# A two-layer hybrid decoder step on one core: page gathers that wait for a sample's exponentials, and recurrence outputs and states in PSUM banks by even and odd head tiles

## The chip, the core and the metric

The kernel runs on one core of one Trainium2 chip. The metric is the device time of one execution in microseconds; the time stated for a kernel is the median of its executions. All arithmetic is fp32.

## What is computed

One inference step of a decoder of 2 layers (width 1024) runs for two groups of tokens at once: a prompt of 256 tokens, and 8 samples of 8 new tokens each, every sample with 2048 past tokens in caches. Each layer is: half a SwiGLU feed-forward block (inner width 2816), a token mixer with three branches, and another half feed-forward block, with RMSNorm around each. Two places of the mixer matter here.

```
# A: RWKV-7 recurrence, 8 heads x 64, with a matrix state s[value, key] per head
def step(s, inp):
    r_t, w_t, k_t, v_t, kk_t, a_t = inp
    sa = einsum('bhvk,bhk->bhv', s, -kk_t)
    s = s * w_t[:, :, None, :] + sa[..., None] * (kk_t * a_t)[:, :, None, :] + v_t[..., None] * k_t[:, :, None, :]
    return s, einsum('bhvk,bhk->bhv', s, r_t)

# C: latent attention, 8 heads; a sample's past latents are paged rows of a pool
ckv  = cache_mla_ckv[l][page_table].reshape(8, 2048, 256)      # latent rows
kr   = cache_mla_krope[l][page_table].reshape(8, 2048, 32)     # rotated keys
s    = (q_lat . ckv + q_rope . kr) * scale                     # 64 rows (8 heads x 8 tokens) x 2048 keys, and 8 own keys
o    = softmax(s) @ ckv
```

Branch B is a dilated window attention over cached keys and values. The new caches, the states and the outputs of both groups are returned.

## The kernel before, in words

Five engines run programs of their own, tied by counted semaphores: TensorE (PE in the profile), VectorE (DVE), ScalarE (ACT), GpSimd (POOL) and SyncE (SP). All matmuls are issued by one helper, `mm` (L787), and all transposes on PE by another, `tr` (L790), so their rows have these lines and are told apart by the names of what they read. SP loads the weights into three slots of `ring`; POOL copies the window caches to the outputs (L722) and issues the page gathers (L740, L744). The order on each engine is the order of the program.

**The recurrence** (PE: `rwkv`, L1023; DVE: L2487 to L2502; ACT: L1866 to L1891). The prompt's 256 tokens are worked in 4 chunks of 64 tokens (g = 0 to 3); a fifth unit holds the samples. Round r of the loop at L1052 builds the products of chunk r and finishes chunk r - 1: `rhs`, `solve` and `outputs` (L1205). Every matmul there is 64 x 64 by 64 columns, on one quarter of the array: `times` (L510) and `beside_each_other` (L1095) pair head tiles so that four quarters work at a time, while `each` (L1088) uses two. Between these steps `fill(n)` (L1002) issues n of the 168 steps of the projections of the other branches (a step is 128 x 128 by 512 columns, or two of half the width for the sample tokens), so that PE has work while DVE and ACT answer. `FILL_STEP` is 2.

`outputs(g)` for g < 4 makes two results for each of 4 head tiles m and both 64-row halves: y (what the chunk puts out) and h (what is added to the state). Before, y is in bank 4 and h in bank 5. The state's part of y comes first, for all tiles and with no wait; then PE waits for U (`u_ev`, from DVE's `u_out`, L2594), multiplies y of even and h of odd tiles, does one step of filling, waits for its own counter `across` (so that two row halves never add to the same bank at once), and does h of even and y of odd tiles. Then it increments `h`. On that, DVE adds h to the state `Hp` and decays it (`state`, L2597 to L2602), and ACT copies y out (L1880, which increments `y_out`). The next `rhs` (L1163) waits for both.

**The latent attention of the samples** (PE: `ml_sample`, L1567; DVE: L2883; ACT: L2037 and L2051; POOL: L746 to L772). One sample b takes one round:
- PE multiplies the scores, `ml_scores(b)` (L1502): 4 steps of low keys, 4 of high keys and 1 of rotary keys, all in 32-row strips. `ml_mm` is incremented after step 5 and after step 8, so it is 2b + 1 within the high keys and 2b + 2 at the end. Then come the result of sample b - 2 by channel, the own tokens of b + 1 (`ml_s`), the products with the values of b - 1 (`ml_pv`), and transposes of the shares of b (`ml_PT`).
- DVE waits for `ml_mm` 2b + 2 and takes the maximum straight from 4 PSUM banks (L2896); four tiny instructions make the bias (L2897 to L2900, `ml_nm`). Then it takes the own scores of b + 1 (L2889), transposes the low keys of sample b + 1 (L2838, `keys`, L2840; these wait for that sample's pages), copies the result of b - 2 (L2922) and the own share (L2908), transposes the high keys of b + 1, and makes the divisor.
- ACT takes the exponentials when `ml_nm` says so (L2042, then L2044 with the increment of `ml_exp`), and copies the transposed shares (L2063).
- POOL gathers the pages of sample b in two halves of 1 MB (L744) and one of rotary keys, 128 KB (L740), into the buffer b modulo 4. For b = 2 and 3 it waits for `ml_mm` to reach b (that is: sample 0's scores are done; sample 1's high keys are under way). From b = 4 on it waits for `ml_pv` b - 3 (the buffer is free) and for `ml_mm` 2(b - 2) + 1 (sample b - 2's high keys are under way). The pages of samples 0 and 1, and the rotary keys of sample 3, are gathered earlier. The second half of sample 2 also waits for the gates' products (`pgm` 24).

`spot`, `spots` and `paired` (L514 to L521) already exist and are used by `rhs` and for the samples: `spot(R, m, at)` is in bank 4 for even m and in bank 5 for odd m.

## Time and profile before

| | us |
|---|---|
| median of 3 executions | 2506.28 |
| lowest and highest | 2504.1, 2511.38 |
| the profiled execution's own time | 2509.38 |
| its span, first to last instruction | 2507.6 |
| PE busy in the span | 2457.0 |
| DVE busy | 1303.8 |
| ACT busy | 562.0 |
| POOL busy | 67.7 |

All times of rows are from the span's start. "Busy" for PE is the time in which a matmul was under way as recorded; the starts of matmuls are recorded, their ends are modelled. `<-remote` behind a wait means that a semaphore's last increment fits no recorded end of an instruction. The mean granted TensorE clock is 0.998 of full speed. The recurrence's chunks run at about 380 to 470 us in layer 0 and 1710 to 1790 us in layer 1, the samples' latent attention at about 850 to 947 and 2093 to 2190 us.

### The profile page before, as it was taken

The page shows a single profiled execution, that of the slowest core. Times are in us where ns is not written, and L with a number is a line of the kernel's source. Part 1 is how long each engine was busy: PE and PEld are TensorE (multiplying, and loading weights), DVE is VectorE, ACT ScalarE, POOL GpSimd, SP SyncE. Part 2 cuts the span into 40 slices and gives each one's busy share as a digit, 9 for nine tenths or more (in the row PEclk, how much of TensorE's full clock was granted, in tenths as well). Part 3 has the DMA queues.
Part 4 walks back from the last instruction along what each step waited for, and adds up shares of the span by engine and source line. Part 5 has one row for each costly group of instructions (what it writes and reads, how often), then busy time and mean ns, then how long its engine had stood idle before and what let it go on. Part 6 is the DMA issues. An engine that isn't in the chain of part 4 may idle for free.

```text
span 2507.6 us, 52981 instructions
## 1 busy us (share of the span) xinstructions
PE 2457.0 (98%) x23140; PEld 2023.9 (81%) x23140; DVE 1303.8 (52%) x2829; ACT 562.0 (22%) x1233; POOL 67.7 (3%) x92
## 2 busy tenths in 40 slices
PE   8999999999999999999999999999999999999998
PEld 7999956666767778999999998566667667799998
DVE  5663554445543563766376545543465335537654
ACT  2110231133432222111121102311344222231111
POOL 0000000000000110000000000000000002000000
PEclk9999999999999999999999999999999999999999
DMA  8767662143986554666856686522549864446775
GB/s 276 248 187 249 215 226 69 53 155 139 394 322 238 159 197 130 202 205 212 262 183 208 209 259 227 166 69 69 182 170 400 293 209 158 179 132 202 235 215 158
DMA packets 260853, 505.59 MB, mean 202 GB/s; under 512 B 9808, under 2 KB 198736, under 8 KB 245648
## 3 DMA queue, kind: packets, MB, share of 16 engines
q1 hardware_dynamic: 251920, 330.77, 40.0%
q0 software_dynamic: 8704, 171.45, 19.0%
q8 instruction: 183, 3.00, 0.5%
q14 instruction: 46, 0.38, 0.0%
HBM read 491.89 MB, written 140.85 MB: 252 GB/s over the span
## 4 chain that ended last, share of the span: by engine, by line
PE 86%; DVE 5%; DMA 4%; ACT 2%; another core or an unknown queue 1%; issue 1%; PEld 1%; SPq 0%; DVEq 0%; ACTq 0%
PE ps L787 82%; PE ps L790 4%; DMA big<-in_cache_swa_k_dram 3%; DVE big L2838 1%; DVE ring L2838 1%; DMA ring<-in_w_in_dram 1%; DVE sml L2896 1%; PEld ps L787 1%; DVE reg L2165 0%; ACT big L1990 0%; DVE reg L2239 0%; ACT reg L1990 0%; DVE x L2157 0%; ACT reg L1931 0%
## 5 line engine op out<-in xcount | busy, mean ns | idle before, releaser
L787 PE MATMUL ps<-reg 128*128 128x160 f32 (+13 forms) x4584 | 504.6, 292 | 1.6 <-DVE reg L2244 1.6
L787 PEld LDWEIGHTS ps<-reg 128*128 128x128 f32 (+5 forms) x4584 | 448.8, 162 | 29.6 <-issue 22.7
L787 PE MATMUL ps<-reg,ring 128*128 128x160 f32 (+2 forms) x3072 | 457.0, 305 | 1.8 <-issue 1.8
L787 PE MATMUL ps<-h,ring 128*128 128x320 f32 (+2 forms) x1984 | 445.7, 376 | 10.9 <-ACT h L1717 8.3
L787 PEld LDWEIGHTS ps<-reg,ring 128*128 128x128 f32 (+1 forms) x3072 | 427.4, 189 | 13.0 <-issue 2.6
L787 PEld LDWEIGHTS ps<-h,ring 128*128 128x128 f32 (+1 forms) x1984 | 322.7, 189 | 98.9 <-issue 22.4
L787 PE MATMUL ps<-ring,h 128*128 128x512 f32 (+3 forms) x896 | 247.0, 468 | 0.0
L787 PEld LDWEIGHTS ps<-big,ring 128*128 128x128 f32 (+2 forms) x1888 | 191.7, 170 | 24.8 <-issue 20.5
L787 PE MATMUL ps<-big,ring 128*128 128x160 f32 (+2 forms) x1888 | 208.4, 284 | 0.5
L787 PEld LDWEIGHTS ps<-ring,h 128*128 128x128 f32 (+1 forms) x896 | 101.8, 163 | 79.9 <-issue 64.8
L787 PE MATMUL ps<-big,reg 32*64 32x256 f32 (+8 forms) x2144 | 130.8, 350 | 1.5 <-DVE big L2838 1.3
L787 PEld LDWEIGHTS ps<-big,reg 32*64 32x64 f32 (+4 forms) x2144 | 99.5, 133 | 27.8 <-issue 15.7
L790 PE MATMUL ps<-cst,big 128*128 128x128 f32 (+1 forms) x672 | 95.2, 281 | 12.6 <-DMA big<-in_cache_swa_k_dram 6.4
L790 PEld LDWEIGHTS ps<-cst,big 128*128 128x128 f32 (+1 forms) x672 | 72.3, 140 | 28.1 <-DMA big<-in_cache_swa_k_dram 8.8
L1827 ACT ACTIVATE reg<-ps 128x320 f32<-128x320 f32 x40 | 17.5, 437 | 316.3 <-PE ps L787 316.3
L787 PE MATMUL ps<-ys,ring 128*128 128x320 f32 x256 | 75.4, 440 | 1.3 <-ACT big L1942 1.2
L787 PEld LDWEIGHTS ps<-big 64*64 64x64 f32 (+1 forms) x1536 | 51.6, 134 | 29.8 <-issue 29.0
L2389 DVE TENSOR_TENSOR ys<-ys,ps 128x320 f32<-128x320 f32 x40 | 19.5, 487 | 107.8 <-PE ps L787 107.7
L787 PEld LDWEIGHTS ps<-ring 128*16 128x16 f32 (+3 forms) x1888 | 59.2, 111 | 15.3 <-issue 15.2
L787 PE MATMUL ps<-ring 128*16 128x128 f32 (+3 forms) x1888 | 71.2, 261 | 0.2 <-issue 0.2
L787 PE MATMUL ps<-ring,reg 32*64 32x256 f32 (+2 forms) x1312 | 70.5, 374 | 0.0
L1830 ACT ACTIVATE ys<-reg 128x640 f32<-128x640 f32 x40 | 29.5, 737 | 181.3 <-DVE reg L2409 181.3
(335 smaller groups left out, 2677.4 us busy)
## 6 DMA issues: line engine op xcount, KB each, us to landing
out_o_swa_k_s_dram<-in_cache_swa_k_dram POOLq DMA_DIRECT2D x16, 4080.0 KB, 15.7
out_o_swa_v_s_dram<-in_cache_swa_v_dram POOLq DMA_DIRECT2D x16, 4080.0 KB, 15.2
ring<-in_w_in_dram SPq DMA_DIRECT2D x30, 2048.0 KB, 8.8
ring<-in_f_wd_dram SPq DMA_DIRECT2D x32, 1408.0 KB, 7.6
ring<-in_f_wg_dram SPq DMA_DIRECT2D x42, 1024.0 KB, 5.7
ring<-in_f_wu_dram SPq DMA_DIRECT2D x42, 1024.0 KB, 8.7
big<-in_cache_swa_k_dram SPq DMA_DIRECT2D x32, 1024.0 KB, 8.9
ring<-in_cache_swa_v_dram SPq DMA_DIRECT2D x32, 1024.0 KB, 7.4
```

The costliest lines, as they stand in the source:

```text
L787: return pe.matmul(out, lhsT, rhs, start=first, stop=last, skip_group_check=True)
L790: return pe.transpose(out, in_, ident[0:rows, 0:rows])
L1827: act.activation(GU[u % 2][:, :, 0, 0:HT], summed(X), ACT.Copy).then_inc(S["gu_act"], 1)
L1830: act.activation(SG[u % 2], GU[u % 2][:, 0], ACT.Sigmoid).then_inc(S["ffn_sg"], 1)
L2389: dve.tensor_tensor(Vs, Xc, Y, ALU.add).then_inc(S["gu_sum"], 1)
L2838: dve.transpose(out, pages).then_inc(S["ml_keys"], 1)
L2896: link(dve.tensor_reduce(sml[:, 0:1], ps[:, 0:4, 0:256], mybir.AxisListType.XY, ALU.max))
```

## The change

POOL: the gathers of sample b >= 2 wait for the exponentials of sample b - 2 (`ml_exp` is b - 1 when ACT is through with them) in place of a count of the score matmuls. The wait for `ml_pv` from b = 4 on stays.

The recurrence: y and h lie in banks 4 and 5 by even and odd tiles (y from column 256, h from column 384). The state's part of y now comes behind the wait for U, odd tiles first; `across` is incremented after the odd ones, four matmuls before the end of that group; PE waits for it, and then does all parts of h and of y without a step of filling between. The step of filling goes to the `fill` behind `outputs`. ACT's copy of y waits for DVE's `state` in place of `h`. DVE reads h through the paired view.

```diff
@@ POOL, the gathers of sample b @@
                     elif b in (2, 3):
                         pool.wait_ge(S["prompt_y"], 2 * H)
                         pool.wait_ge(S["ml_prep"], 1)
-                        pool.wait_ge(S["ml_mm"], b)
+                        pool.wait_ge(S["ml_exp"], b - 1)
                     else:
                         pool.wait_ge(S["ml_pv"], b - 3)
-                        pool.wait_ge(S["ml_mm"], 2 * (b - 2) + 1)
+                        pool.wait_ge(S["ml_exp"], b - 1)
@@ PE, the rounds of the recurrence @@
                     if r:
                         outputs(r - 1)
-                    fill(FILL_STEP - FILL_STEP // 2 if 0 < r < 5 else FILL_STEP)
+                    fill(FILL_STEP)
                     if r < 5:
                         blocks(r)
@@ PE, outputs(g) for g < 4 @@
-                y, h = [lambda R, m, bank=bank: ps[R, bank, col(m, at=256)] for bank in (4, 5)]
-                y_of_u = lambda R, Q, m: mm(y(R, m), U[Q, m], RB[i][Q, m], False, False)
-                y_of_v = lambda R, Q, m: mm(y(R, m), VB[i][Q, m], KKRK[i][Q, m, CHUNK:], False, True)
-                h_of_u = lambda R, Q, m: mm(h(R, m), VB[i][Q, 4 + m], U[Q, m], m < 2, False)
-                h_of_v = lambda R, Q, m: mm(h(R, m), KDr[i][Q, m], VB[i][Q, m], False, True)
-                each(lambda R, m: mm(y(R, m), Hp[R, m], RqT[R, m, t], m == 0, False))
                 pe.wait_ge(S["u_ev"], g + 1)
-                beside_each_other(y_of_u, h_of_u)
-                beside_each_other(y_of_v, h_of_v).then_inc(S["across"], 1)
-                fill(FILL_STEP // 2)
+                for m in (1, 3, 0, 2):
+                    for r in range(2):
+                        R = channels(r)
+                        q = mm(spot(R, m, 256), Hp[R, m], RqT[R, m, t], m < 2, False)
+                    if m == 3:
+                        q.then_inc(S["across"], 1)
                 pe.wait_ge(S["across"], ACROSS["outputs", g])
-                beside_each_other(h_of_u, y_of_u)
-                beside_each_other(h_of_v, y_of_v).then_inc(S["h"], 1)
+                y_of_u = lambda R, Q, m: mm(spot(R, m, 256), U[Q, m], RB[i][Q, m], False, False)
+                y_of_v = lambda R, Q, m: mm(spot(R, m, 256), VB[i][Q, m], KKRK[i][Q, m, CHUNK:], False, True)
+                h_of_u = lambda R, Q, m: mm(spot(R, m, 384), VB[i][Q, 4 + m], U[Q, m], False, False)
+                h_of_v = lambda R, Q, m: mm(spot(R, m, 384), KDr[i][Q, m], VB[i][Q, m], False, True)
+                for part in (h_of_u, h_of_v, y_of_u, y_of_v):
+                    q = beside_each_other(part, part)
+                q.then_inc(S["h"], 1)
@@ ACT @@
                     if 1 <= r < 5:
-                        act.wait_ge(S["h"], g + 1)
-                        act.activation(S_[8][:, :, g * CHUNK:(g + 1) * CHUNK], ps[:, 4, 256:512].rearrange("p (m t) -> p m t", m=4), ACT.Copy).then_inc(S["y_out"], 1)
+                        act.wait_ge(S["state"], g + 1)
+                        act.activation(paired(S_[8][:, :, g * CHUNK:(g + 1) * CHUNK]), spots(256), ACT.Copy).then_inc(S["y_out"], 1)
@@ DVE @@
             def state(g):
                 dve.wait_ge(S["h"], g + 1)
-                link(dve.tensor_tensor(Hp, quarter(5, 256), Hp, ALU.add))
+                link(dve.tensor_tensor(paired(Hp), spots(384), paired(Hp), ALU.add))
```

## Rows read from the trace of the kernel before

**Rows 1.** The page: the chain that ended last, by engine.

```profile
PE 86%; DVE 5%; DMA 4%; ACT 2%; another core or an unknown queue 1%; issue 1%; PEld 1%; SPq 0%; DVEq 0%; ACTq 0%
```

**Rows 2.** Windows, core 0: us, PE, PEld, DVE, ACT, POOL busy, PEclk, DMA share, GB/s.

```profile
396.00:470.00 74.00, 73.38 (x1346) 47.19 (x1345) 33.42 (x103) 10.90 (x23) 0.00 (x0) 1.00 0.23 80
851.10:928.40 77.30, 72.90 (x1364) 55.73 (x1365) 59.97 (x137) 21.95 (x56) 16.00 (x17) 1.00 0.58 209
2094.20:2174.40 80.20, 74.38 (x1364) 57.49 (x1363) 59.94 (x137) 22.09 (x56) 16.00 (x17) 0.98 0.56 202
```

**Rows 3.** DVE's waits over the whole span: us in total, times, longest.

```profile
DVE sml L2896 <- remote: 23.2, 9, 4.3
```

**Rows 4.** Timeline, layer 0, samples 3 and 4: start us, us, engine, line.

```profile
883.28 0.64 PE L787 MATMUL ps<-big 32*64 32x256 f32 x16
883.47 0.94 POOL L744 DMA_INDIRECT reg<-in_cache_mla_ckv_dram,pidx  x1 [8.36 <-PE ps L787]
884.71 0.93 POOL L744 DMA_INDIRECT reg<-in_cache_mla_ckv_dram,pidx  x1 [0.30 <-issue]
885.60 1.23 DVE L2896 TENSOR_REDUCE sml<-ps 128x1 f32<-128x1024 f32 x1 [2.35 <-remote]
897.36 1.23 DVE L2896 TENSOR_REDUCE sml<-ps 128x1 f32<-128x1024 f32 x1 [2.32 <-remote]
```

**Rows 5.** Timeline, layer 0, samples 0, 6 and 7, no gather begun before.

```profile
850.39 0.64 PE L787 MATMUL ps<-big 32*64 32x256 f32 x16
851.13 1.22 DVE L2896 TENSOR_REDUCE sml<-ps 128x1 f32<-128x1024 f32 x1 [3.80 <-PE ps L787]
917.88 1.22 DVE L2896 TENSOR_REDUCE sml<-ps 128x1 f32<-128x1024 f32 x1 [0.77 <-PE ps L787]
920.04 2.37 DVE L2838 STREAM_TRANSPOSE ring<-ring 128x1024 f32<-128x1024 f32 x2
928.42 1.22 DVE L2896 TENSOR_REDUCE sml<-ps 128x1 f32<-128x1024 f32 x1 [1.43 <-PE ps L787]
```

**Rows 6.** Timeline, layer 0, sample 0: ends of exponentials, a gather, ACT beside it.

```profile
854.39 0.19 ACT L2044 ACTIVATION_READ_ACCUMULATOR ring<-ring,sml 64x1 f32 x1
855.26 0.94 POOL L744 DMA_INDIRECT h<-in_cache_mla_ckv_dram,pidx  x1 [1.17 <-PE ps L787]
856.06 0.60 ACT L2063 ACTIVATE reg<-ps 128x512 f32<-128x512 f32 x1 [0.51 <-PE ps L790]
```

**Rows 7.** The gathers' lines (L744, then L740), from issue to landing.

```profile
DMA to landing us min/median/max: 5.6/7.0/9.4
...
DMA to landing us min/median/max: 5.0/6.7/7.7
```

**Rows 8.** Timeline, layer 0: the low keys of sample 2.

```profile
864.79 1.25 DVE L2838 STREAM_TRANSPOSE ring<-ring 128x1024 f32<-128x1024 f32 x1 [0.30 <-DVE ring L2889]
```

**Rows 9.** PE's timeline, chunk 0 of layer 0: from before outputs to behind it.

```profile
404.14 1.98 PE L787 MATMUL ps<-ring,h 128*128 128x512 f32 x4
407.44 0.57 PE L787 MATMUL ps<-reg,big 64*64 64x64 f32 x14
408.47 1.12 PE L787 MATMUL ps<-ring,h 128*128 128x512 f32 x2
409.53 0.27 PE L787 MATMUL ps<-big,ring 64*64 64x64 f32 x2
411.21 0.68 PE L787 MATMUL ps<-big,ring 64*64 64x64 f32 x16
```

**Rows 10.** PE's timeline, chunk 0 of layer 0: rhs, with its wait inside.

```profile
399.82 0.63 PE L787 MATMUL ps<-ring 64*64 64x64 f32 x16
400.29 0.46 PE L787 MATMUL ps<-big,reg 64*64 64x64 f32 x16
```

**Rows 11.** Timeline, chunk 0 of layer 0: DVE's U, and ACT's next wait behind y.

```profile
404.33 0.42 DVE L2594 TENSOR_SCALAR big<-ps 128x256 f32<-128x256 f32 x1 [0.79 <-PE ps L787]
414.93 0.38 ACT L1885 ACTIVATE big<-ps 128x256 f32<-128x256 f32 x1 [4.26 <-PE ps L787]
```

## The prediction

> **What bounds the kernel now.** I read the chain first: 86% of it is PE [rows 1], so whatever makes PE's work shorter counts, and elsewhere only what keeps PE waiting. Then the windows of the two stages that the change touches [rows 2]. In the recurrence PE is busy for 73.38 of 74 us, with DVE at 33.42: PE is the bound, and only its own time counts. In the samples' latent attention, from the first maximum (L2896) to the eighth, a layer takes 77.3 us and the other 80.2, and PE, with 72.90 and 74.38, isn't quite the bound. Something else sets the pace there.
>
> DVE's waits name it [rows 3]: L2896 waited 9 times, 23.2 us in all, for something "remote", that is for an increment that fits no end of a matmul. The timeline shows one [rows 4]: the last score matmuls begin at 883.28 and end 0.64 later, at 883.92, but the maximum begins at 885.60, 1.7 us behind. Where no gather has just begun it doesn't wait like this [rows 5]: the same matmuls from 850.39 end at 851.03, and the maximum starts 0.10 later. In between lies POOL: its two latent gathers were issued at 883.47 and 884.71 [rows 4], and the second is over at 885.64, as the maximum starts (0.04 off; samples 1 to 4 of layer 0 and 1 to 5 of layer 1 are alike, the nine of rows 3). The maximum stands in a ring: maximum, low keys, high keys, scores, next maximum. So I take it that PE's increment reaches DVE late while gathers are being issued, and that each time costs about 1.6 us. The pace agrees: 885.60 to 897.36 is 11.76 us [rows 4], and without gathers 917.88 to 928.42 is 10.54 [rows 5].
>
> **The gathers, part by part.** Now a sample's gathers begin within the scores of sample b - 2, just ahead of the critical increment. Afterwards they begin when ACT's exponentials end, 854.58 where the maximum began at 851.13 [rows 5, 6]: 3.45 us behind a maximum. POOL then issues until about 7 us behind it (three, 1.24 apart [rows 4]), and the next critical increment comes 10 us behind it.
>
> Removed: the late start, nine times. The trace has the new place once: a gather is issued at 855.26, until 856.20, and ACT's copy of the transposed shares, released by PE's increment, starts at 856.06 with no such delay [rows 6]. If an increment there came late, it would be that of the shares' transposes; ACT's copy is needed only one score group later, some 6 us, which covers it.
>
> Added: the pages are asked for later, and the low keys (DVE, in order, with high keys, own share and divisor queued behind, and PE's scores waiting for them) need them 2.16 us behind the next maximum (917.88 to 920.04 [rows 5]). The rotary gather is third, 2.5 us behind the first, and lands 5.0, 6.7 or 7.7 us after its issue (minimum, median, maximum [rows 7]), so a set lands L = 7.5, 9.2 or 10.2 us after it begins. From the low keys to the next maximum are 8.38 us (920.04 to 928.42 [rows 5]). Two samples then take at least 3.55 + 9.2 + 8.38 = 21.1 us, 10.6 each, beside the 10.54 of PE and DVE without gathers: the two limits meet, and I take 10.55. With 10.2 it is 11.1; with 7.5 the undisturbed 10.5 stays, and at best somewhat less.
>
> Sample 2 is the tight one. Before, its low keys began at 864.79, after a wait of 0.30 [rows 8]. Afterwards its rotary keys are asked for at 854.7, the second latent half 2.5 us later, at 857.2, and that lands 5.6, 7.0 or 9.4 us later [rows 7]: 862.8, 864.2 or 866.6. With the median the keys begin at 864.2, and the maximum of sample 2 comes some 8.0 us later (the 8.38 is from a round in which PE had a full load), at 872.2. Five more at 10.55 end at 925.0, against 928.42: 3.4 us gained in layer 0. Layer 1 has the same work: from 80.2 to 73.9 (925.0 less 851.1), 6.3 gained. It was longer because one more sample was delayed and because its clock stands at 0.98 [rows 2], 1.6 us of full clock lost; I assume that this dip came from the stalls and goes. In all 9.7 us. Bounds: with all the longest landings 2.4 are lost at sample 2 and 2.8 in five rounds, a layer, so 9.7 - 10.4 = -0.7; with the shortest, and rounds of 10.0, 9.7 + 2 x (1.2 + 2.8) = 17.7. After the eighth maximum the same chain follows and simply starts earlier.
>
> A rule of the Trainium skill speaks against the removal: by "SBUF — State Buffer", section "Who interferes with whom", a VectorE reduction never contends with GpSimd on this chip, and TensorE and ScalarE wait for nobody. By it the coincidence in [rows 4] would be no cause and the gathers' part would be worth 0. The trace so far stands against it with the 1.7 us beside 0.10; it is a rival below.
>
> **The recurrence, part by part.** The number of matmuls and of filling steps is the same. What goes is one interruption of each `outputs`, in 4 chunks of 2 layers, 8 times. A fill of one step occupies PE for 1.12 us, one of two steps for 1.98 [rows 9]: 2 x 1.12 - 1.98 = 0.26 saved. Going into and out of a fill once less saves some 0.05 more, as the first small matmuls behind one last 0.27 [rows 9]. Added is PE's wait for its own `across` with only four matmuls behind the increment. `rhs` has the same pattern: its first 16 records start at 399.82 and those behind the wait at 400.29 [rows 10], 0.47 us for 16, or 0.03 each, with the wait hidden within; for the slower first pair behind it I take 0.05. Net 0.26, say 0.25, of the 3.77 from 407.44 to 411.21 [rows 9], so 8 x 0.25 = 2.0 us. Bounds: the wait drains a matmul of 0.27 each time, 0; or it is free, 0.31 x 8 = 2.5, which I widen to 3.
>
> At nothing: the wait for U now stands ahead of the state's part; U is out at 404.75 (404.33 + 0.42 [rows 11]), 2.7 us ahead of 407.44 [rows 9]; without that cover it would cost what U is late. ACT's wait for `state` is about 0.9 us longer (two adds or multiplies of DVE), but `h` comes about 1.1 earlier, without the fill before it; and ACT's next wait lasts 4.26 us [rows 11]. DVE's state starts earlier; its own next wait for `blocks` grows. Nothing on PE waits for either.
>
> **Sum.** 9.7 + 2.0 = 11.7 us against the profiled execution's own 2509.38 (span 2507.6): 2497.7. That execution is 3.1 above the median 2506.28, so on the median 2494.6; I say 2494.5.
>
> **Rivals.**
> 1. *The late start isn't POOL's.* Whatever delays the increment follows the dense scores themselves, and the maxima still start 1.7 us late; the pages land in time for rounds of 11.8. For it: sample 5 of layer 0 started in time with a gather just begun, and I don't know the mechanism. Against it: samples 0, 6 and 7, with the same matmuls and no gather, are on time. It leaves only the recurrence: 2506.3 - 2.0 = 2504.3.
> 2. *The pages come late: slower.* It decides in DVE's wait at the low keys. Rounds are as slow as before when 3.55 + L + 8.38 = 23.5, so from L = 11.6. With L = 14 (a set stuck behind another, as all landings add up) a round is 13.0, 5 x 1.2 = 6 more a layer than before, and sample 2 some 4 more: 2506.3 + 20 - 2 = 2524. Against it: the longest L by [rows 7] is 10.2, and the DMA queues are busy for 0.58 of the stage [rows 2]. It needs a landing beyond any row.
> 3. *The recurrence gains nothing*, because PE drains at `across`: 2496.5.
>
> **Numbers.** About 0.3% (7.5 us) is what a measurement of this kernel can tell from no change. Chances: my forecast 0.68; rival 1 0.16; rival 2 0.06; rival 3 0.10. Within the forecast, long landings or a dip of the clock that stays leave less than 7.5 in about one case of eight. Faster by more than 0.3%: 0.60 + 0.07 = 0.67. Within: 0.16 + 0.08 + 0.01 and part of rival 2, 0.26. Slower: 0.07, rival 2 at its full price and unforeseen waits. The range: down to 2487, most of the bounds of both parts (-17.7 and -3 would be 2485.6); up to 2504.5, to take in rival 1.
>
> **What would show it.** Right: no "remote" wait of L2896, its starts 0.1 behind the last score matmul; gathers issued about 3.5 us behind a maximum; rounds of 10.5; windows from first to eighth maximum near 74 us in both layers; from 407.44 to `blocks` about 3.5 us. Wrong: rounds still of 11.8 with POOL moved (rival 1); a wait of DVE at L2838 for a gather of over 1 us in every round (rival 2); an idle gap of PE behind the state's part of y (rival 3); a new late increment in front of ACT's L2063 that something waits for.

## The result, and the profile after

| | before | after |
|---|---|---|
| median | 2506.22 us (4 runs) | 2525.44 us (4 runs) |
| lowest and highest | 2504.1, 2511.38 | 2523.2, 2541.48 |
| profiled execution, its span | 2509.38, 2507.6 | 2523.2, 2521.4 |

The ratio is 1.0078, with a 95% interval of 1.0054 to 1.0102: slower by 19 us, where I had forecast 12 us less. Lines of the code from L1218 on stand two lines lower in the kernel after: L2896 is L2898 now, L2838 is L2840, L2889 is L2891.

First the windows of the stages of [rows 2], the latent attention again from the first maximum to the eighth (us, then PE, PEld, DVE, ACT, POOL busy, PEclk, DMA share, GB/s):

```profile
393.00:467.00 74.00, 73.32 (x1319) 47.07 (x1317) 33.44 (x102) 10.90 (x23) 0.00 (x0) 1.00 0.25 87
848.10:935.90 87.80, 77.29 (x1365) 61.42 (x1365) 60.29 (x138) 22.17 (x56) 16.00 (x17) 0.98 0.50 185
2100.80:2188.30 87.50, 77.83 (x1365) 61.73 (x1365) 60.84 (x137) 22.19 (x56) 16.00 (x17) 0.98 0.50 185
```

The stages have grown from 77.3 and 80.2 us to 87.8 and 87.5, 17.8 us together: this is where the loss is. Then the seven distances from maximum to maximum, from the timelines of both kernels (not rows, but differences of them):

```
                before                                       after
layer 0   11.2 11.5 11.8 11.8 10.6  9.9 10.5     11.5 11.9 11.8 11.8 12.6 11.9 16.3
layer 1   11.2 13.1 11.8 11.8 11.8 10.2 10.4     11.5 11.8 12.3 11.8 12.6 11.8 15.9
```

Two things stand out: the middle rounds still take 11.8 or more, and the last one takes 16. DVE's waits (total us, times, longest) name the second. In place of the "remote" of [rows 3], which is gone, there is:

```profile
DVE ring L2840 <- DMA ring<-in_cache_mla_krope_dram,pidx: 9.9, 2, 5.2
DVE ring L2840 <- DMA h<-in_cache_mla_ckv_dram,pidx: 4.5, 2, 2.3
DVE ring L2840 <- DMA reg<-in_cache_mla_krope_dram,pidx: 1.3, 2, 0.7
DVE ring L2840 <- DMA big<-in_cache_mla_krope_dram,pidx: 0.4, 1, 0.4
```

L2840 is the low keys, and all of them wait for pages: 16.1 us. The timeline of layer 0 shows the longest, that of sample 7:

```profile
912.32 0.94 POOL L744 DMA_INDIRECT ring<-in_cache_mla_ckv_dram,pidx  x1 [9.58 <-issue]
914.80 0.95 POOL L740 DMA_INDIRECT ring<-in_cache_mla_krope_dram,pidx  x1 [0.30 <-issue]
919.59 1.23 DVE L2898 TENSOR_REDUCE sml<-ps 128x1 f32<-128x1024 f32 x1 [2.75 <-PE ps L787]
926.91 2.37 DVE L2840 STREAM_TRANSPOSE ring<-ring 128x1024 f32<-128x1024 f32 x2 [5.19 <-DMA ring<-in_cache_mla_krope_dram,pidx]
935.90 1.22 DVE L2898 TENSOR_REDUCE sml<-ps 128x1 f32<-128x1024 f32 x1 [2.03 <-PE ps L787]
```

The set was asked for at 912.32 and complete at 926.83: L = 14.5 us, where the longest of before gave 10.2 [rows 7]. The DMA view of 911 to 930 us says what lay beside it (queues: packets, MB, share of 16 engines; then issues with KB and median us to landing):

```profile
q0 software_dynamic: 368, 2.36, 29.8%
q1 hardware_dynamic: 528, 2.10, 28.4%
...
big<-in_w_branch_c_dram SPq DMA_DIRECT2D x1, 2048.0 KB, 13.1
ring<-in_cache_mla_ckv_dram,pidx POOLq DMA_INDIRECT x2, 11.1
ring<-in_cache_mla_krope_dram,pidx POOLq DMA_INDIRECT x1, 12.0
```

SP's load of the branch's weights (L683, 2 MB) waits for `ml_pv` 5, which comes at 912.47, within 0.2 us of the first gather. The two shared the engines half and half. Before, the gathers had begun at 907.39, 4.9 us ahead of the load, and had landed at 917.55. While DVE waits, PE stands for 4.4 us, and right behind that its granted clock is down, at half speed (1.2 GHz) for most of the next 4 us; the last round of layer 1 is alike, with 3.9 us of standing:

```profile
930.00:934.00 4.00, 4.00 (x89) 2.70 (x96) 3.66 (x9) 0.71 (x2) 0.00 (x0) 0.58 0.01 2
```

The middle rounds are told by PE's timeline between the maxima at 883.31 and 895.09:

```profile
883.31 1.23 DVE L2898 TENSOR_REDUCE sml<-ps 128x1 f32<-128x1024 f32 x1 [2.42 <-PE ps L787]
...
887.53 0.94 POOL L744 DMA_INDIRECT reg<-in_cache_mla_ckv_dram,pidx  x1 [8.35 <-ACT ring L2046]
889.09 1.94 PE L787 MATMUL ps<-ring,reg 32*64 32x256 f32 x44
890.01 0.95 POOL L740 DMA_INDIRECT reg<-in_cache_mla_krope_dram,pidx  x1 [0.30 <-issue]
891.80 0.88 PE L787 MATMUL ps<-ring,reg 32*64 32x256 f32 x18 [0.77 <-issue]
892.53 1.32 PE L787 MATMUL ps<-big,reg 32*64 32x256 f32 x38
895.09 1.23 DVE L2898 TENSOR_REDUCE sml<-ps 128x1 f32<-128x1024 f32 x1 [2.29 <-PE ps L787]
```

The matmuls of the low keys (x44, x18) wait for nothing, yet PE starts none between 890.65 and 891.80. The stop begins 0.6 us behind the start of the third issue (890.01) and outlasts it. All ten sets of three issues (the pages of samples 2 and 4 to 7, in both layers) have this stop, 1.15 to 1.18 us between two starts, some in two pieces; the two sets of sample 3, whose rotary keys are gathered earlier and which have two issues, have none. The maxima themselves now begin 0.04 to 0.13 behind the last score matmul. The price was moved, not removed.

The recurrence did what was forecast. PE's timeline of chunk 0, for [rows 9]:

```profile
406.56 0.63 PE L787 MATMUL ps<-reg,big 64*64 64x64 f32 x16
...
408.12 1.98 PE L787 MATMUL ps<-ring,h 128*128 128x512 f32 x4
410.04 0.68 PE L787 MATMUL ps<-big,ring 64*64 64x64 f32 x16
```

From the state's part of y to `blocks` it is 3.48 us against 3.77.

**Where the 19 us are.** Page waits +16.1; ten stops in place of nine late increments, about +1.6 (each costs a round some 1.6 to 1.9, see the experiments); recurrence 8 x 0.29 = -2.3. These make +15.4. The spans of the two profiled executions differ by 13.8 (the one before took 3.2 more than its median, the one after 2.2 less), the medians by 19.2. This is an account of two traces and no proof that the terms add up; the experiments test the two large ones.

### The profile page after: what moved, and what is told of

Read it like the earlier page. It is cut to its first block, busy times and chain, and to the rows that moved or that the text cites. A ratio compares the mean times of both kernels' runs of the same rounds, so it can differ in the third digit from the quotient of the medians.

```text
span 2521.4 us, 52981 instructions
## 1 busy us (share of the span) xinstructions
PE 2461.2 (98%) x23140; PEld 2033.8 (81%) x23140; DVE 1305.8 (52%) x2829; ACT 562.2 (22%) x1233; POOL 67.7 (3%) x92
## 4 chain that ended last, share of the span: by engine, by line
PE 89%; DMA 5%; DVE 2%; ACT 2%; issue 1%; PEld 1%; POOL 0%; SPq 0%; DVEq 0%; POOLq 0%; ACTq 0%
PE ps L787 84%; PE ps L790 4%; DMA big<-in_cache_swa_k_dram 2%; DMA ring<-in_cache_mla_krope_dram,pidx 1%; DMA h<-in_cache_mla_ckv_dram,pidx 1%; DMA ring<-in_w_in_dram 1%; PEld ps L787 1%; DVE reg L2167 0%; ACT big L1992 0%; ACT reg L1992 0%; DVE reg L2241 0%; POOL ring L744 0%; DVE ring L2840 0%; DVE sml L2898 0%; ACT reg L2044 0%
## 5 line engine op out<-in xcount | busy, mean ns | idle before, releaser
L787 PEld LDWEIGHTS ps<-big,reg 32*64 32x64 f32 (+4 forms) x2144 | 105.4, 134 | 20.5 <-issue 16.0
L790 PE MATMUL ps<-cst,big 128*128 128x128 f32 (+1 forms) x672 | 95.2, 281 | 13.1 <-DMA big<-in_cache_swa_k_dram 6.9
L787 PE MATMUL ps<-ring,reg 32*64 32x256 f32 (+2 forms) x1312 | 84.4, 400 | 6.9 <-issue 6.5
L787 PEld LDWEIGHTS ps<-ring,reg 32*64 32x64 f32 (+1 forms) x1312 | 51.6, 139 | 31.7 <-issue 23.8
```

What stands on the lines that cost most here:

```text
L787: return pe.matmul(out, lhsT, rhs, start=first, stop=last, skip_group_check=True)
L790: return pe.transpose(out, in_, ident[0:rows, 0:rows])
```

## The experiments

The runs stood on five chips, here called A to E. Each ratio is against the kernel before on the same chip. Its median was there:

| chip | kernel before, us | runs |
|---|---|---|
| A | 2509.4 | experiment 1 |
| B | 2507.7 | `no_gathers_from_4`, `one_gather_from_4`, `rows_of_half_length`, `behind_own_scores` |
| C | 2509.6 | `two_gathers_from_4`, `before_no_gathers_from_4`, `pages_behind_own_scores_load_later`, `recurrence_alone_2` |
| D | 2497.9 | `own_scores_rows_of_half_length`, `halves_apart`, `halves_apart_load_later` |
| E | 2498.3 | experiment 5 |

The five kernels of experiment 2, `own_scores_rows_of_half_length` and `before_again` were run once each, for their traces.

**1. Which half, and the last pages.** Four kernels. `recurrence_alone` has only the recurrence's diff, `gathers_alone` only POOL's. The others are the kernel after with

```diff
+ last_pages_as_before
                         pool.wait_ge(S["ml_pv"], b - 3)
-                        pool.wait_ge(S["ml_exp"], b - 1)
+                        if b == 7:
+                            pool.wait_ge(S["ml_mm"], 2 * (b - 2) + 1)
+                        else:
+                            pool.wait_ge(S["ml_exp"], b - 1)
+ load_held_back
-                        sp.wait_ge(S["ml_pv"], 5)
+                        sp.wait_ge(S["ml_pv"], 6)
```

> The kernel before with the recurrence's edit alone; POOL's gathers wait for counts of the score matmuls as before. Theory A (the two parts are independent; the recurrence gives about 0.3 us in each of 8 chunks, as the offsets between the traces of before and after say, and the whole loss lies in the gathers): 2506.2 - 2.2 = about 2504, between 2503 and 2505. Rival (the recurrence's edit changes where later work lies, and some of the loss is its own): over 2506.

> The kernel before with the gathers' edit alone. Theory A: all of the loss is here, 10.4 us in layer 0 and 7.2 in layer 1 by the offsets between the two traces; with other layer-1 parts some 19 to 22 us over before: 2525 to 2528. Rival: near before, 2506, if the loss came from both together.

> The kernel after, but sample 7's gathers wait for the score matmuls of sample 5 as before (some 5 us earlier than the exponentials of sample 5). Theory A (the last round of each layer waits for these pages: DVE waited 5.2 and 4.7 us for them, PE stood idle as long, because they run at the same time as the 2 MB load of the branch's weights): these waits go, 2525.4 - 9.9 = about 2515.5, and the landing of sample 7's last page comes back to about 10 us behind the first gather. Rival (the load isn't to blame and the pages of any sample land late when asked for behind another's): the wait shrinks by less than half, over 2520.

> The kernel after, but the 2 MB load of the branch's weights waits for the values of sample 5 (ml_pv 6) in place of those of sample 4, so that it starts some 12 us later. Theory A (the load and sample 7's gathers share the DMA queues and each slows the other): sample 7's pages land some 10 us behind the first gather instead of 14.5, the waits of 5.2 and 4.7 us go, about 2515.5; the load is needed only by the branch's matmuls behind sample 7's shares. Rival 1 (the gathers are slow by themselves at this place): no change, 2525. Rival 2 (the load then comes too late for PE): PE waits for the branch's weights behind the shares, a loss there that takes back part of the gain, 2518 to 2525.

Measured: `recurrence_alone` 2504.1, ratio 0.9993 (0.997 to 1.0017); `gathers_alone` 2527.4, 1.0073 (1.0049 to 1.0098); `last_pages_as_before` 2515.38, 1.0022 (1.0004 to 1.0041); `load_held_back` 2517.71, 1.0021 (1.0003 to 1.0039). So the loss is POOL's edit alone, and the overlap of sample 7's pages with the load is about half of it: against `gathers_alone` on the same chip, and with the 2.3 us of the recurrence taken off, the two ways of parting them give back 9.7 and 7.4 us. With the load held back, sample 7's set landed 10.1 and 9.8 us behind its first issue, not 14.5. DVE's waits there:

```profile
DVE ring L2840 <- DMA ring<-in_cache_mla_ckv_dram,pidx: 4.7, 2, 2.4
```

This is what stays of page waits of over 1 us a piece; the 5.2 for sample 7 is gone (0.8 is left in layer 0). One thing more is in the trace of `last_pages_as_before`: with sample 7's set back at its old place, just ahead of a critical increment, the late increment came back too. The maximum of sample 5 begins 0.95 us behind the last score matmul in layer 0 and 2.43 in layer 1 (a round of 14.8).

**2. What keeps the round at 11.8.** The kernel after with fewer or shorter gathers for samples 4 to 7 (they work on older pages in part or whole, with DVE's counts of landings set to match):

```diff
@@ no_gathers_from_4 @@
-                for b in range(NB):
+                for b in range(4):
@@ one_gather_from_4: the first latent half alone @@
+                    if b >= 4:
+                        latents_gathered(b, 0)
+                        continue
@@ two_gathers_from_4: no rotary keys @@
-                    if b >= 4:
-                        krope_gathered(b)
@@ rows_of_half_length, in latents_gathered (cut) @@
+                    if b >= 4:
+                        short = io["cache_mla_ckv"].rearrange("l n (s r) c -> (l n s) (r c)", s=32)
+                        ... out=KRc[b % 4][half][:, 0:4, :] ...
```

> The kernel after without the gathers of samples 4 to 7: those samples work on the pages of samples 0 to 3 again, so the output is another; it is a measurement. Theory B (a gather's issuing costs PE and DVE some time in its round wherever it stands, 1.3 us a round, and this is what keeps the round at 11.8): the four rounds that no longer issue anything (from the third maximum on) take 10.0 to 10.5 us in place of 11.8 to 16, and the four late increments or stops of PE are gone. Rival (the pace of 11.8 is PE's and DVE's own and has nothing to do with gathers): these rounds still take 11.5 or more, and only the last, which waited for pages, shrinks.

> The kernel after with only the first latent half of samples 4 to 7 gathered (half the bytes, one of three issues; the rest of the pages is that of an earlier sample, so the output is another). Theory B with a price by issue: rounds lie at about 10.4 + 0.4, near 10.9. If only the third issue hurts (PE stopped 3.1 to 4.3 us behind the start of the first, when the third was being issued): 10.4, as without gathers. Rival (the bytes in flight hurt): about 11.1, half way.

> The kernel after with as many gathers as ever, at the same places, but the latent ones of samples 4 to 7 bring rows of half the length (half the bytes; the other half of the buffer keeps older data, so the output is another). Theory B (issuing hurts, bytes don't): the middle rounds stay at 11.8, PE still stops within the low keys; the last round of each layer no longer waits for its pages and also takes about 11.8. Rival (traffic hurts): the middle rounds fall to about 11.

> The kernel after without the rotary gather of samples 4 to 7 (two issues a sample in place of three, 2 MB of 2.13; the rotary keys are those of an earlier sample, so the output is another). Theory C (PE's stop within the low keys is bound to the third issue, which is under way when it begins): the stop goes, the middle rounds take about 10.2. Rival (any issue does it, the stop only comes with the second then, or the price is by the issue): the stop stays or halves, rounds of 11 or more.

> The kernel before without the gathers of samples 4 to 7 (those samples work on older pages, so the output is another). Theory B (the late increments of the kernel before are the same thing as the stops of PE in the kernel after: what POOL's issuing costs at another place): no late increment from the third maximum on, rounds of about 10.0, and the span is 2 x 4 x 1.6 us or so shorter than before, some 2497. Rival (late increments come from the dense scores): rounds of 11.8 as before.

`before_no_gathers_from_4` is the same first edit in the kernel before. The maxima of two samples without gathers, in the kernel after and in the kernel before:

```profile
886.81 1.22 DVE L2898 TENSOR_REDUCE sml<-ps 128x1 f32<-128x1024 f32 x1 [0.85 <-PE ps L787]
896.77 1.23 DVE L2898 TENSOR_REDUCE sml<-ps 128x1 f32<-128x1024 f32 x1 [0.84 <-PE ps L787]
```

```profile
2120.87 1.23 DVE L2896 TENSOR_REDUCE sml<-ps 128x1 f32<-128x1024 f32 x1 [0.84 <-PE ps L787]
2130.83 1.23 DVE L2896 TENSOR_REDUCE sml<-ps 128x1 f32<-128x1024 f32 x1 [0.84 <-PE ps L787]
```

9.96 us both times, eight rounds of the one kernel and nine of the other between 9.96 and 10.4 (2501.35 and 2496.52 us in all). Where the gathers are gone, late increments and stops are gone; the sets that are left in these two kernels still have theirs (1.7 us and 1.17, once a layer). So both are the price of gathers. With half the bytes but all three issues the stop stays (PE's timeline of `rows_of_half_length`; the third issue begins at 880.75), and the middle rounds are 11.75 to 11.87. The last ones missed their expectation with 13.9 and 12.3: sample 7's pages still made DVE wait 2.9 and 2.4 us.

```profile
879.76 1.99 PE L791 MATMUL ps<-ring,reg 32*64 32x256 f32 x44
882.52 0.89 PE L791 MATMUL ps<-ring,reg 32*64 32x256 f32 x18 [0.78 <-issue]
```

With two issues (1 MB each) it is gone, and a round without another trouble takes 10.33; with one, 10.13, in a run of 2506.91 us (`two_gathers_from_4`, DVE and PE; its lines stand lower by two):

```profile
2150.40 1.23 DVE L2896 TENSOR_REDUCE sml<-ps 128x1 f32<-128x1024 f32 x1 [3.83 <-PE ps L785]
2156.11 2.21 PE L785 MATMUL ps<-ring,reg 32*64 32x256 f32 x60
2160.73 1.23 DVE L2896 TENSOR_REDUCE sml<-ps 128x1 f32<-128x1024 f32 x1 [0.97 <-PE ps L785]
```

So it is the issuing, not the bytes, and in the low keys it is the third issue in a row. Late increments need only two: when the critical one is due, the third gather isn't yet begun [rows 4]. Yet as a whole the run with two gathers took 2521.56 us, hardly less than the kernel after: other rounds took 11.0 to 13.8, and one 15.6. Its DVE waited 11.2 us for pages, and PE had three stops of 2.2 to 2.3 us of another kind, which the third experiment shows.

**3. Another place, and a second kind of stop.** All gathers from sample 2 on wait for the own scores (`ml_s` is b). From sample 3 on their first issue comes 1.2 to 3.1 us behind a maximum, when PE is in the products with the values; sample 2's comes 5.1 behind one:

```diff
+ behind_own_scores, for b = 2, 3 and for b >= 4
-                        pool.wait_ge(S["ml_exp"], b - 1)
+                        pool.wait_ge(S["ml_s"], b)
```

> The kernel after with another place for the gathers: from sample 2 on they wait for the own scores (ml_s is b), whose increment comes about 1.2 us behind the maximum's start, so that a gather starts about 2 us behind a maximum in place of 4.2, when PE is in the products with the values and nobody waits for an increment of PE for 3 us. Theory B: the stop of PE, 3.1 to 4.3 us behind the first issue, falls on the transposes of the shares ahead of the low keys, where PE's order has no slack either: rounds stay near 11.8, but the pages come 2.2 us earlier and the waits of the last rounds shrink by as much: 2525.4 - 5 = about 2520. If the stop belongs to the low keys alone (32-row matmuls), it goes: rounds of 10.5, and with the pages of sample 7 still against the load the time is about 2505.

2511.85 us, ratio 1.0017 (1.0 to 1.0034): less gained than the better branch of the expectation, though its mechanism came out. From sample 3 on there is no stop in the low keys, and the quiet rounds take 10.11 (2151.59 to 2161.70). Sample 2's three issues still fall on low keys: there the stop stands in both layers, the granted clock is at half speed right behind it (0.51 from 858.0 to 861.5), and these first rounds take 14.0 each, against 11.2 before. On chip D the same issues stand at the same place (`own_scores_rows_of_half_length`, which shortens rows only from sample 4 on) and there is no stop; the round takes 9.6. The low keys of sample 1 in layer 1, on chip B and on chip D:

```profile
2099.41 3.23 PE L787 MATMUL ps<-ring,reg 32*64 32x256 f32 x57
2103.43 0.48 PE L787 MATMUL ps<-ring,reg 32*64 32x256 f32 x4 [0.79 <-issue]
```

```profile
2098.75 1.98 PE L791 MATMUL ps<-ring,reg 32*64 32x256 f32 x64
```

Two more rounds of layer 0 take 13.0 and 12.5. PE's timeline in the second, and the queues of 904.2 to 905.3 us:

```profile
903.62 1.28 PE L787 MATMUL ps<-big,reg 32*64 32x256 f32 x38
906.70 0.42 PE L787 MATMUL ps<-big,reg 32*64 32x256 f32 x1 [1.80 <-issue]
```

```profile
q0 software_dynamic: 92, 0.37, 85.3%
q8 instruction: 1, 0.02, 5.6%
q14 instruction: 1, 0.01, 2.1%
```

PE stops inside a step of the high keys. At 904.21 one packet of 16 KB moves in the instruction queue, until 905.20, and PE goes on 1.50 us later. The latent attention of the twenty profiles has 51 such stops of 0.8 us and more, at nine places of the program, all in the 32-row scores or within about 2 us behind them (for instance in the scores of sample 5, and behind those of sample 3), and in each a 16 KB packet ends 1.2 to 1.6 us ahead of the restart. The 1.15 us stops have, but for one, no such packet at that distance. With none of the gathers from sample 4 on, the packet of the place in sample 5's scores begins 2.6 us ahead of it and the place costs 0.2; here it began 0.3 ahead. That PE stands for its next instructions is inferred from this coincidence; no run moved the packets alone. Full queues are not the whole of it either: `no_gathers_from_4` has one such stop, of 1.01 us, in the scores of sample 7, 55 us behind the last gather, with nothing in the DMA queues between 2160 and 2165 us but two instruction packets:

```profile
2164.70 0.68 PE L787 MATMUL ps<-big,reg 32*64 32x256 f32 x14 [0.63 <-issue]
```

The kernel before has one too, in layer 1, and right behind it the granted clock is down to 0.57 for 4 us:

```profile
2106.07 0.37 PE L787 MATMUL ps<-reg,ring 128*64 128x128 f32 x2 [1.79 <-issue]
2106.44 4.82 PE L787 MATMUL ps<-big,reg 128*64 128x256 f32 x28
```

```profile
2106.00:2110.00 4.00, 3.93 (x23) 3.22 (x24) 3.81 (x10) 1.49 (x4) 0.00 (x0) 0.57 0.95 391
```

The two together are its round of 13.1. `recurrence_alone` stops at the same place for 1.5 us between two starts in place of 2.1, without a fall of the clock: its products with the values take 3.6 us in place of 4.8, and the round 11.2.

The Trainium skill ("Runtime: NRT & Kernel Launch", section "Instruction fetch mechanics") says that each engine streams its instructions by DMA in blocks of 16 KiB and that this is mostly hidden. The packets agree with the blocks; that it is mostly hidden doesn't hold for the samples' latent attention of this kernel, if the 51 stops above, from 0.8 to 3.8 us, are waits for instructions.

**4. Trying for a version that beats both.** Three placements on the kernel after, and the recurrence's half again:

```diff
+ pages_behind_own_scores_load_later: b = 2 on ml_mm b as before, else ml_s b, and
-                        sp.wait_ge(S["ml_pv"], 5)
+                        sp.wait_ge(S["ml_pv"], 6)
+ halves_apart: b = 2 as before, b = 3 on ml_s b, and for b >= 4
                         pool.wait_ge(S["ml_pv"], b - 3)
-                        pool.wait_ge(S["ml_exp"], b - 1)
...
                         latents_gathered(b, half)
+                        if b >= 4 and half == 0:
+                            pool.wait_ge(S["ml_s"], b)
```

> A version meant to beat both: the kernel after, with the gathers from sample 3 on waiting for the own scores (ml_s is b), that of sample 2 for the score matmuls as before, and the 2 MB load held to ml_pv 6. Theory B: no stop of PE in the low keys, no late increment, no page wait of sample 2 (3.8 a layer less than the run with all pages behind the own scores) nor of sample 7: 2511.9 - 2 x 2.5 - 3 = about 2504, ratio to before 0.998 or a little under. Rival (stops move to other places, such as PE's supply of instructions during the gathers): 2508 or more, ratio 1.000 or more.

> The recurrence's edit alone once more, in more rounds, beside the version above: the offset of 0.3 us in each of 8 chunks says a ratio of 0.9991; the gathers as before, so the rest is unchanged.

> The run with the gathers behind the own scores, once more, but the latent gathers of samples 4 to 7 bring rows of half the length (output another). Theory D (PE's stops of 1.4 to 2.2 us wait for its next 16 KB of instructions, whose load is held up by the pages' bytes in the DMA queues): with half the bytes the stops at the scores of samples 4 and 6 shrink to under 0.8 us, the rounds from sample 3 on are 10.1 to 10.8, and the span falls by 6 us or more from 2507.1, since the waits for pages go too. Rival (the stops come with POOL's issuing): gaps of 1.5 and 2.2 us as before, span over 2504.

> A version meant to beat both: the kernel after, with sample 2's gathers as before, those of sample 3 behind the own scores, and from sample 4 on the first latent half as soon as its buffer is free (ml_pv b - 3, in the round before), the second half and the rotary keys behind the own scores (ml_s b). Never more than two issues at a time, and 1 MB at two places of a round instead of 2 MB at one. Theory D: shorter queues, instruction loads on time, rounds of 10.1 to 10.4, no page wait: 2506.3 - 2.2 - about 8 = 2496, ratio 0.996. Rival (an issue in the low and high keys delays the critical increment again, or stops remain): 2504 or more.

> The same with the 2 MB load of the branch's weights held to ml_pv 6. Theory D: the pages of sample 7 and the load no longer overlap, and it is 1 to 3 us shorter than the other, about 2494, unless sample 7's pages were in time anyway (then equal) or the load now delays an instruction load (then slower by the 2 to 4 us of such a stop).

`pages_behind_own_scores_load_later` missed: 2514.3 us, 1.0014 (0.9995 to 1.0034), with instruction stops of 1.4 to 3.8 us, the longest while the load held back ran. `recurrence_alone_2`: 2507.1, 0.9979 (0.9963 to 0.9994), the only version whose interval lies below 1; that of its first run, on chip A, includes 1. `own_scores_rows_of_half_length` bore out half of its expectation: at the two places the stops shrank from 1.46 to 0.51 and from 2.17 to none, but the span fell by only 2 us: sample 2's pages made DVE wait 9.8 us in the two layers. It stood on another chip, so half the bytes aren't the only difference. `halves_apart`: 2497.08, 1.0005 (0.9989 to 1.0022); `halves_apart_load_later`: 2497.3, 0.9993 (0.998 to 1.0006). The rounds of `halves_apart` are 9.6 to 11.4 us, as hoped; the profiled execution of the other has a second round of 14.6 and 12.9, with instruction stops of 2.7 and 1.8 us. Neither gains over before, and the load held back didn't bring the 1 to 3 us expected of it. That made me look at the kernel before on such a chip.

**5. The same kernels again, on a chip where before takes 2498.**

> The kernel before once more, for a profile on the same chip as the two runs beside it. If the stages of latent attention vary little from execution to execution: 77 and 77 to 80 us from the first maximum to the eighth, rounds of 11.8 while gathers are issued. If PE's instruction stops fall at random: a stage of 77 to 82 with the difference in one round of 12 to 14.

> The kernel after once more. The loss doesn't depend on the chip (it is a place in the program order): ratio 1.006 to 1.009, rounds of 11.8 and a last round of about 16 in each layer. Rival (the wait for sample 7's pages is a matter of one execution): a ratio under 1.005.

> The version with the halves apart once more. Theory D: on a chip where the kernel before takes some 2507 it gains about 10 us, ratio 0.996. Rival (what it gains in the latent attention is given back in other places or by stops of PE in most executions): within 0.15% of before, ratio 0.9985 to 1.0015, as on the chip of the first comparison.

The kernel before, line for line, with a gather begun ahead of a maximum as in [rows 4], and its two windows (first to eighth maximum):

```profile
891.02 0.64 PE L787 MATMUL ps<-big 32*64 32x256 f32 x16
891.21 0.94 POOL L744 DMA_INDIRECT ring<-in_cache_mla_ckv_dram,pidx  x1 [7.46 <-PE ps L787]
...
891.76 1.23 DVE L2896 TENSOR_REDUCE sml<-ps 128x1 f32<-128x1024 f32 x1 [1.77 <-PE ps L787]
```

```profile
851.40:924.30 72.90, 70.60 (x1365) 57.57 (x1365) 60.01 (x138) 22.09 (x56) 16.01 (x17) 1.00 0.61 222
2099.10:2171.20 72.10, 70.65 (x1364) 56.65 (x1365) 59.96 (x138) 22.04 (x56) 16.01 (x17) 1.00 0.62 225
```

The scores end at 891.66 and the maximum starts 0.10 behind: no late increment, here or in any round of it, though the gathers are issued at the same place and take the same 0.94 us. What was expected of it, windows of 77 and 77 to 80 us, missed: 72.9 and 72.1 us replace 77.3 and 80.2.

So the late increments and the 1.15 us stops are a thing of some chips; I can't say of what in them. The late increments are in every profile of the old place from the first comparison, A and C (nine each in `before`, `recurrence_alone` and `recurrence_alone_2`), and in none of the sixteen maxima of `before_again`. Of the sets whose third issue falls among 32-row matmuls, 52 of 53 have the stop (0.7 us and more between two starts) in the first comparison and on A, B and C; on D it is none of 2, on E none of 6. The rest of D's gathers stand at places that can't be compared. One execution was profiled of each kernel, so the split by chips rests on this pattern and on the medians: the difference of the two windows, 12.5 us, is of the size of the difference of the medians, 8 to 12. The profiled execution of `before_again` itself took 2506.15 us, 8 more than the median of its chip: between the layers, at 1484, PE stood for 8.4 us while a weight load was awaited (DVE waited 14.0 for it), with the granted clock at 0.50 in the 10 us behind 1487, and it lost there what it had gained here.

`after_again` took 2522.95 us, ratio 1.0093 (1.007 to 1.0116), a little over the range expected, and by another split: no 1.15 us stops, a first round of 9.6 (11.5 in the profile after) and quiet ones of 10.1, but DVE waits 15.0 us for pages in all, and PE has four instruction stops of 2.1 to 2.6 us between starts. The last rounds, expected at 16, take 10.4 and 11.9. The second take 16.0 and 14.9: DVE waits 4.7 and 4.1 us for the pages of sample 2, which are needed sooner where nothing else holds PE up. The other waits are for samples 4, 5 and 7.

```profile
DVE ring L2840 <- DMA h<-in_cache_mla_ckv_dram,pidx: 8.8, 2, 4.7
```

`halves_apart_2`: 2499.1, ratio 1.0006 (0.9991 to 1.0021). It heals the change and gains nothing here, where there is no late increment to save. Whether it gains on a chip that has them wasn't run.

## Why the prediction was wrong, step by step

- **The late start is POOL's issuing: right.** Without gathers it is gone (experiment 2), and rival 1 falls; its one point, sample 5 of layer 0, was itself 0.5 us late. What I took for a property of the kernel belongs to some chips, which one trace can't show (experiment 5).
- **"Removed: the late start, nine times": the first step that failed.** I checked the new place by one increment ("with no such delay"), beside a gather that stood alone, where three in a row were to come; and I looked for increments that might come late. What came was no late increment but a stop of PE itself within matmuls that wait for nothing, 1.15 us, at the third issue of a set. The 6 us of cover that I named for a late transpose were none for that. Rounds: 11.8 measured, 10.55 forecast. In the first comparison the term was worth +1.6 us, not part of -9.7.
- **"need them 2.16 us behind the next maximum ... L = 7.5, 9.2 or 10.2": the second step that failed, and the dearer one.** Three sizes were off. The first issue comes 4.22 us behind a maximum (883.31 to 887.53), where the sum had 3.55: POOL needs 0.77 from the end of the exponentials to the issue. L was 9.9 to 10.3 in the middle rounds. With these two my own sum gives 4.22 + 10.0 + 8.38 = 22.6 us for two samples, 11.3 a round in place of 10.55, so most of the gain was gone even without the stop; `after_again`, which has no such stop, waits 15.0 us for pages. And two sets don't simply share what is free: the last met the 2 MB load, landed after 14.5 and 14.3 us, and made DVE wait 5.2 and 4.7. The rows were of a schedule in which the gathers ran ahead of that load. I had moved them past SP's queue without asking what SP issues then; `ml_pv` 5 was in the code.
- **Rival 2** had named the mechanism, the place (DVE's wait at the low keys) and L = 14 and got 0.06, because "It needs a landing beyond any row". That its 2524 is so near to the measured 2525.4 is luck: it has 13.0 us in every round and late landings throughout, where the runs show a stop of PE in the middle rounds and such a landing in the last of each layer alone.
- **Sample 2:** its keys were forecast 13.1 us behind the first maximum (864.2 less 851.1) and began 16.0 behind it (864.09 less 848.10), 2.9 late: POOL's issues stood 0.7 later than I had them, and the second half landed after 8.8 us, where I took 7.0. That is within the 9.4 of the bounds, but it ate the gain of the round. The waits were 2.3 and 2.2 us in the two layers, and in `after_again` they are the dearest of all.
- **The clock's dip in layer 1:** I assumed that it came from the stalls and would go. It did follow a stop of PE, the instruction stop of 2.1 us, and that one is absent in the profile after by chance. But the profile after has a granted clock of 0.98 in both stages: each layer has a dip behind its long page wait.
- **The undisturbed pace** was smaller than the 10.54 that I took from the last round [rows 5]: 9.96 without gathers.
- **The recurrence: right**, 0.29 us a chunk for 0.25, 2.3 us for 2.0; by the two comparisons 1.8 and 5.3 us, intervals 12 and 8 wide, so that the size rests on the traces.
- The Trainium skill's rule ("SBUF — State Buffer", section "Who interferes with whom"), which I weighed as a rival, isn't contradicted: the maximum took 1.22 or 1.23 us in every row, and what was late was the order of PE's work or its signal. That TensorE waits for nobody is said there of the ports of SBUF; it stood all the same, and no run shows for what.

## What to carry to other kernels

A transfer that is asked for later is to be held against everything that will then be issued beside it, on every queue, at the new time; the longest landing of the old schedule is no bound. If a stall vanishes where an engine is busy issuing, ask what that engine's issuing does at the new place to work that waits for nothing, not only to the signals there. And a stall that decides a forecast is worth a second profile from another chip before it is counted as the kernel's own.

## What the runs showed of the hardware

- Indirect gathers issued in a row, 1.24 us apart, can hold PE up. Two of them just ahead of an increment made it arrive 1.6 to 2.4 us late; the third of three stopped 32-row matmuls that wait for nothing for 1.15 us; beside 128-row products with the values three cost 0.15 us a round (10.11 for 9.96). Two in a row don't stop the low keys, and half the bytes change nothing. Late increments and stops were not seen on chip E, nor the stop on chip D. The cause is open.
- In the 32-row scores and shortly behind them PE can stand for 0.8 to 3.8 us, and each time a 16 KB packet of the instruction queue ends 1.2 to 1.6 us ahead of the restart. The longest stop (3.8) stood beside the 2 MB load, which had 87% of the DMA engines' time; one of 1.0 stood with the queues empty. What makes the packets late is open.
- Behind several stands of PE of 1.5 to 4.4 us the granted clock was at half speed for the next few us, so that a wait costs more than its own length: matmuls with the values took 4.8 us in place of 3.6. It didn't follow every such stand (`halves_apart` has one of 2.0 us between two starts without it).
